# First expert weights sent in three earlier pieces, router sums in column groups, first gather on token rows: one change to a hybrid decoder step

## The chip, the cores and the metric

The kernel runs on one core of one Trainium2 chip. The metric is the device time of one launch, in microseconds (us), as the median of several runs. Engine names are those of the profile: PE is TensorE's matmul, PEld its weight load, DVE is VectorE, ACT is ScalarE, POOL is GpSimd, SP is SyncE; SPq is SP's queue, from which the large DMA transfers are issued.

## The reference

The reference is one layer of a decoder on 288 tokens (256 prompt tokens, 8 sequences of 4 sample tokens), width 1024, all in float32. Attention and a state-space block run side by side, an output projection joins them, and a mixture of 32 experts follows, of which each token uses four:

```
merged = concat[_rmsnorm(attn, ...), _rmsnorm(ssm_o, ...)]
x = x + merged @ lp['w_out']
xn2 = _rmsnorm(x, lp['norm_ffn_g'])
y_ff = _moe(xn2, w_router, b_router, w_gate_up, b_gate_up, w_down, b_down)
x = x + y_ff
...
logits = x2d @ w_router + b_router          # 32 experts
top_v, top_i = lax.top_k(logits, TOP_K)     # 4 of them
gates = softmax(top_v)
h = xb @ w_gate_up[e] + b_gate_up[e]        # 1024 -> 2048
out = _clamped_swiglu(h) @ w_down[e] + b_down[e]
```

The expert weights are 32 x (8 MB + 4 MB), and every one of them is read once in a launch.

## The kernel before, in words

Each engine has its own list of instructions, written out by hand in program order; semaphores (`wait_ge`, `then_inc`) are all that ties the lists together. Nothing reorders them.

**First part.** Activations stand transposed in `xT` (8 tiles of 128 channels x 288 tokens). PE makes the input projection, attention (`score`, `turn`, `values`) and the state-space block (`outputs(0)` to `outputs(3)`). Then come three stretches of 32 matmuls each: the first half of `w_out` on the attention half, `w_glu`, and the second half of `w_out` ("outB", eight tiles m = 0 to 7). For each outB tile DVE scales and adds (`v_rot`, `xT`, `xg`, lines 1676 to 1679) and ACT squares the new `xT` tile into `x2sq`; PE adds the squares up through a matrix of ones (`square(k)`, one matmul after each tile, in bank 4).

**Router.** After the last tile PE makes the logits: `w_r` is the moving operand, the tokens are the stationary one (3 token blocks of 96 x 8 channel tiles). The mean square is turned into 1/rms on all 128 rows (`r2`), transposed to token rows (`rt`), and the token-row copies `x_tok` of the normalised input are made by transposes and ACT copies. DVE picks the four best experts of each token (`lg`, `v8`, `eq`, `sel`), PE counts places (`pos_ready`), DVE builds `oh`, the 0/1 matrix of the tokens of the first expert, and PE gathers those tokens (`gather_first`). After `oh`, DVE goes on with the order in which the experts are to be processed (`ord_e`, semaphore `order_ready`).

**Experts.** Each of 32 experts is processed once, on 64 or 32 token slots ("mid" 64, "few" 32, "many" 64 and 32). Weights come in blocks of 1 MB: 8 blocks of gate/up weights in `gu_ring` and 4 of down weights in `dn_ring`, whose 8 slots hold two experts. `gate_up` uses the gate/up blocks one after the other and gives each slot free with `gu_used`; `down` does so with `dn_used`.

**SP's queue** sets when weights are sent. `load_first` sends the first 16 blocks (all of `gu_ring` and `dn_ring`) once `glu_done` has reached 8, because the rings lie on memory that the first part uses. `load_others` waits for `order_ready`, reads three expert numbers, and then sends the remaining 368 blocks one by one, each when its slot is free: for the first of them SP waits for `gu_used` >= 1. SP issues in program order, so a wait holds up everything behind it.

The profile's lines of `mm` all read L474 (its only `matmul` call); groups are told apart by the tiles they read.

## Time and profile before

| | |
|---|---|
| median of 3 runs | 1167.56 us (1161.33 to 1170.48) |
| time of the profiled execution | 1161.27 us |
| its span, first to last instruction | 1159.4 us |
| mean granted TensorE clock | 0.968 |
| PE busy | 1042.1 us (90%) |
| DVE busy | 411.0 us (35%) |
| ACT busy | 200.9 us (17%) |
| read from HBM | 419.86 MB |

The page gives busy times per engine, the span in 40 slices, the chain that ended last, and groups of instructions. The first sixth of the span is the first part and the router; the rest is the 32 experts. A busy share is no bound by itself: here PE and the DMA engines are both nearly full through the experts, and what matters is which of them waits for the other.

### The profile page before, as it was taken

The page shows a single profiled execution, that of the slowest core. Times are in us where ns is not written, and L with a number is a line of the kernel's source. Part 1 is how long each engine was busy: PE and PEld are TensorE (multiplying, and loading weights), DVE is VectorE, ACT ScalarE, POOL GpSimd, SP SyncE. Part 2 cuts the span into 40 slices and gives each one's busy share as a digit, 9 for nine tenths or more (in the row PEclk, how much of TensorE's full clock was granted, in tenths as well). Part 3 has the DMA queues.
Part 4 walks back from the last instruction along what each step waited for, and adds up shares of the span by engine and source line. Part 5 has one row for each costly group of instructions (what it writes and reads, how often), then busy time and mean ns, then how long its engine had stood idle before and what let it go on. Part 6 is the DMA issues. An engine that isn't in the chain of part 4 may idle for free.

```text
span 1159.4 us, 17080 instructions
## 1 busy us (share of the span) xinstructions
PE 1042.1 (90%) x6475; PEld 448.8 (39%) x6475; DVE 411.0 (35%) x886; ACT 200.9 (17%) x425; POOL 2.7 (0%) x6
## 2 busy tenths in 40 slices
PE   6977899999998999889988998879999999999995
PEld 5755777533233323332332233223333333333332
DVE  6898525323132313231323122223333333222223
ACT  3296423011011101110111111011111111111110
POOL 0000000000000000000000000000000000000000
PEclk9966999799999999999999999999999999999997
DMA  9511039799999999999999999999999999999994
GB/s 360 158 42 73 7 124 423 295 377 421 420 395 422 421 421 422 422 421 422 422 422 421 422 422 421 421 421 421 420 421 421 421 423 422 421 423 421 422 421 186
DMA packets 63303, 425.01 MB, mean 367 GB/s; under 512 B 8196, under 2 KB 10884, under 8 KB 13344
## 3 DMA queue, kind: packets, MB, share of 16 engines
q1 hardware_dynamic: 61488, 422.23, 88.5%
q10 hardware_dynamic: 1728, 2.11, 0.5%
q8 instruction: 25, 0.41, 0.1%
q0 software_dynamic: 48, 0.15, 0.0%
q14 instruction: 14, 0.11, 0.0%
HBM read 419.86 MB, written 2.51 MB: 364 GB/s over the span
## 4 chain that ended last, share of the span: by engine, by line
PE 76%; DVE 9%; DMA 9%; issue 3%; ACT 2%; SPq 1%; ACTq 1%; DVEq 0%
PE banks L474 72%; DMA gu_ring<-w_gu_dram 9%; DVE xT L1813 2%; DVE raw L1767 1%; PE banks L824 1%; PE banks L786 1%; ACT gath L1209 1%; PE banks L877 1%; DVE hl L1779 1%; DVE hT L1784 1%; SPq L319 1%; PE banks L884 0%; PE banks L831 0%; ACT raw_s L1253 0%; DVE hl L1776 0%
## 5 line engine op out<-in xcount | busy, mean ns | idle before, releaser
L474 PE MATMUL banks<-gu_ring,xe 128*64 128x512 f32 x1408 | 324.5, 603 | 4.9 <-DMA gu_ring<-w_gu_dram 4.2
L1813 DVE TENSOR_TENSOR xT<-xT,banks 128x576 f32<-128x576 f32 x132 | 93.6, 751 | 487.6 <-PE banks L474 487.6
L474 PEld LDWEIGHTS banks<-gu_ring,xe 128*64 128x64 f32 x1408 | 95.2, 138 | 198.9 <-issue 182.5
L474 PE MATMUL banks<-dn_ring,hT 128*64 128x512 f32 x704 | 157.7, 596 | 3.5 <-DVE hT L1784 3.5
L474 PE MATMUL banks<-gu_ring,xe_s 128*32 128x512 f32 x896 | 110.6, 600 | 7.4 <-DMA gu_ring<-w_gu_dram 7.4
L474 PEld LDWEIGHTS banks<-dn_ring,hT 128*64 128x64 f32 x704 | 47.9, 137 | 94.6 <-issue 88.7
L474 PE MATMUL banks<-gT,ye 64*128 64x288 f32 x352 | 57.8, 439 | 12.7 <-DVE xT L1813 12.7
L1224 ACT ACTIVATE raw<-banks 128x512 f32<-128x512 f32 x22 | 13.1, 597 | 294.4 <-PE banks L474 294.4
L474 PE MATMUL banks<-x_tok,oh 96*64 96x512 f32 x252 | 58.7, 601 | 0.0
L474 PE MATMUL banks<-dn_ring,hT_s 128*32 128x256 f32 x896 | 55.6, 396 | 2.7 <-ACT xe_s L1243 2.7
L1767 DVE COPY raw<-banks 128x512 f32<-128x512 f32 x22 | 15.2, 692 | 107.4 <-PE banks L474 107.4
L474 PEld LDWEIGHTS banks<-gu_ring,xe_s 128*32 128x32 f32 x896 | 22.2, 108 | 76.5 <-issue 58.3
L474 PEld LDWEIGHTS banks<-gT,ye 64*128 64x128 f32 x352 | 28.7, 185 | 49.9 <-DVE xT L1813 29.3
L1233 ACT ACTIVATE ye<-banks 128x512 f32<-128x512 f32 x22 | 13.1, 597 | 159.2 <-PE banks L474 159.2
L474 PEld LDWEIGHTS banks<-dn_ring,hT_s 128*32 128x32 f32 x896 | 28.0, 113 | 31.5 <-issue 17.4
L474 PE MATMUL banks<-xg,w_in 128*128 128x288 f32 x160 | 39.8, 406 | 0.0
L474 PE MATMUL banks<-aT,w_out 128*128 128x288 f32 x128 | 34.0, 420 | 3.3 <-issue 3.3
L474 PE MATMUL banks<-gT_s,ye_s 32*128 32x288 f32 x224 | 22.1, 464 | 15.7 <-DVE xT L1813 15.1
L474 PEld LDWEIGHTS banks<-xg,w_in 128*128 128x128 f32 x160 | 30.4, 190 | 8.4
L824 PE MATMUL banks<-ident,raw 128*128 128x128 f32 x176 | 28.9, 287 | 4.7 <-DVE raw L1767 4.7
L474 PEld LDWEIGHTS banks<-aT,w_out 128*128 128x128 f32 x128 | 25.1, 198 | 10.6 <-issue 3.6
L824 PEld LDWEIGHTS banks<-ident,raw 128*128 128x128 f32 x176 | 18.4, 140 | 27.8 <-issue 18.0
(338 smaller groups left out, 858.9 us busy)
## 6 DMA issues: line engine op xcount, KB each, us to landing
gu_ring<-w_gu_dram SPq DMA_DIRECT2D x256, 1024.0 KB, 24.0
dn_ring<-w_dn_dram SPq DMA_DIRECT2D x128, 1024.0 KB, 21.9
w_out<-w_out_dram SPq DMA_DIRECT2D x2, 2048.0 KB, 7.9
w_in<-w_in_dram SPq DMA_DIRECT2D x3, 1024.0 KB, 15.9
w_in<-w_in_dram SPq DMA_DIRECT2D x4, 512.0 KB, 10.2
W<-W1c SPq DMA_DIRECT2D x16, 128.0 KB, 2.3
w_glu<-w_glu_dram SPq DMA_DIRECT2D x1, 2048.0 KB, 8.5
xT<-xT_dram SPq DMA_DIRECT2D x2, 576.0 KB, 5.6
```

Source lines behind the costliest of these rows:

```text
L319: sp.dma_start(gu_ring[k][:], a["w_gu"][bass.ds(x, 1), k].rearrange("o p f -> (o p) f")).then_inc(gu_in[k], 16)
L474: return nc.tensor.matmul(out, lhsT, rhs, start=start, stop=stop, **kw)
L786: last = pe.transpose(pb[6][:, c * P:(c + 1) * P], gath[:, c * P:(c + 1) * P], ident[:])
L824: last = pe.transpose(pb[2 + part][:, c * P:(c + 1) * P], raw[:, part, c * P:(c + 1) * P], ident[:])
L877: last = pe.transpose(pb[7][:, t * MT:(t + 1) * MT], goh[0:MT, t], ident[0:MT, 0:MT])
L1209: A(gath[:], pb[5][:], ACT.Copy).then_inc(S("gath_ready"), 1)
L1224: A(raw[:, 0], pb[0][:], ACT.Copy).then_inc(S("g_copied"), 1)
L1233: A(ye[:], pb[4][:], ACT.Copy, scale=0.5).then_inc(S("ye_ready"), 1)
L1767: X.tensor_copy(raw[:, 1], pb[1][:]).then_inc(S("l_copied"), 1)
L1779: X.scalar_tensor_tensor(out=hl[:], in0=hl[:], scalar=1.0, in1=hg[:], op0=ALU.add, op1=ALU.mult).then_inc(S("h_step"), 1)
L1784: X.scalar_tensor_tensor(out=hT[:], in0=th[:], scalar=1.0, in1=hl[:], op0=ALU.add, op1=ALU.mult).then_inc(S("h_ready"), 1)
L1813: X.tensor_tensor(two, two, pair[(1, 3)[n % 2]].rearrange("p (h f) -> p h f", h=2)[:, :, 0:T], ALU.add).then_inc(S("acc_done"), 1)
```

## The change

Four things are moved or written anew.

1. **Loads.** The first 16 blocks go in three pieces: six gate/up blocks when `an_ready` is 4 (the attention half is normalised), four down blocks behind the load of the second half of `w_out`, and the last six (two gate/up, four down) where all 16 went before.
2. **Router.** Squares and logits become matmuls with a 32-column stationary operand, each in one of four column groups of the array (`tile_position`); the partial sums of the four groups lie in the four row quarters of banks 4 and 7. They are done in two halves, after tile 5 and after tile 7. The logits' moving operand is now `xg`. ACT copies the sums to `sumT`, DVE the logits to `lgT`, and matmuls with `fold` (a 0/1 matrix) add the four quarters and turn the result to token rows in one step. 1/rms is then taken on 96 x 3 numbers instead of 128 x 288.
3. **First gather.** `gather_first` is gone; the first expert uses the same `gather(0)` and `turn_gathered(0)` as the later ones: 12 matmul passes on token rows, an ACT copy to `gath`, four transposes, an ACT copy to `xe`.
4. **Fillers and setup.** `busy(bank, src, n)` issues n matmuls whose result nobody reads: 4 ahead of `outputs(0)`, 2 ahead of the first gather, 1 ahead of its transposes and 1 after them. DVE's constants for the experts (12 small instructions) are made before the outB tiles instead of after them.

```
+        sp.wait_ge(S("an_ready"), CT)
+        first_gu(sp, range(0, 6))
         sp.wait_ge(S("outA_done"), KT)
         sp.dma_start(w_out[:], a["w_out"][:, CT:2 * CT]).then_inc(S("wout_in"), 16)
+        sp.wait_ge(S("y_done"), 4)
+        sp.wait_ge(S("hlast_ready"), 2)
+        first_dn(sp, 0)
 
         sp.wait_ge(S("glu_done"), 8)
         sp.wait_ge(S("out_done"), 64)
-        load_first(sp)
+        first_gu(sp, range(6, 8))
+        first_dn(sp, 1)
...
+        def busy(bank, src, n):
+            for _ in range(n):
+                mm(pb[bank][:, 0:src.shape[1]], ident[:], src, True, True)
...
+        busy(4, xT[:, 0, 0:2 * P], 4)
         pe.wait_ge(S("tz_ready"), 16)
         pe.wait_ge(S("hin_ready"), 2)
         outputs(0)
...
-        def square(k):
-
-            if k == 0:
+        def router_part(h):
+
+            def square(q):
+                pe.wait_ge(S("x2sq_ready"), 4 * h + q + 1)
+                return mm(pb[4][NE * q:NE * q + NE, 0:T], ones[:, 0:NE], x2sq[:, q], h == 0, h == 1,
+                          tile_position=(0, NE * q))
+
+            def logit(q):
+                k, g = 4 * h + q, (q + 1) % 4
+                pe.wait_ge(S("xn_ready"), k + 1)
+                return mm(pb[7][NE * g:NE * g + NE, 0:T], w_r[:, k], xg[:, k], h == 0, h == 1, tile_position=(0, NE * g))
+
+            if h == 0:
                 pe.wait_ge(S("sv_ready"), 1)
...
-            if m >= 2:
-                square(m - 2)
-        square(KT - 2)
-        square(KT - 1)
+            if m == 5:
+                router_part(0)
+        router_part(1)
...
-        for t, (f, n) in enumerate(MTS):
-            for k in range(KT):
-                last = mm(pb[5][0:n, t * NE:(t + 1) * NE], xg[:, k, f:f + n], w_r[:, k], k == 0, k == KT - 1)
+        def fold_rows(bank, src, n):
+            for t, (f, w) in enumerate(MTS):
+                last = mm(pb[bank][0:w, t * n:(t + 1) * n], src[:, f:f + w], fold[:, 0:n], True, True)
             last.then_inc(S("logits_ready"), 1)
...
         pe.wait_ge(S("xtok_ready"), 6)
+        busy(0, xg[:, 0, 0:2 * P], 2)
...
-        gather_first()
+        gather(0)
+        busy(0, xg[:, 0, 0:2 * P], 1)
+        turn_gathered(0)
+        busy(0, xg[:, 0, 0:2 * P], 1)
```

On SP's queue, from the load of `w_glu` to the wait for the expert order. Before:

```order
L438 DMA w_glu<-w_glu_dram 128x4096 [waits x_ready]
L440 DMA w_out<-w_out_dram 128x4096 [waits outA_done]
L328 DMA gu_ring_49<-w_gu_dram 128x2048 [waits out_done,glu_done]
L328 DMA gu_ring_50<-w_gu_dram 128x2048
L328 DMA gu_ring_51<-w_gu_dram 128x2048
```

After:

```order
L442 DMA w_glu<-w_glu_dram 128x4096 [waits x_ready]
L330 DMA gu_ring_49<-w_gu_dram 128x2048 [waits an_ready]
L330 DMA gu_ring_50<-w_gu_dram 128x2048
L330 DMA gu_ring_51<-w_gu_dram 128x2048
L330 DMA gu_ring_52<-w_gu_dram 128x2048
L330 DMA gu_ring_53<-w_gu_dram 128x2048
L330 DMA gu_ring_54<-w_gu_dram 128x2048
L446 DMA w_out<-w_out_dram 128x4096 [waits outA_done]
L335 DMA dn_ring_57<-w_dn_dram 128x2048 [waits hlast_ready,y_done]
```

Six expert blocks now stand ahead of `w_out`'s second half and four behind it.

On PE, from the end of outB to the expert's first gather. Each row's tiles are written banks<-moving or stationary operands, the shape is that of the result. Before:

```order
L474 MATMUL banks<-aT,w_out 128x288 x3
L474 MATMUL banks<-x2sq,ones 128x288 [waits x2sq_ready] x3
L474 MATMUL banks<-w_r,xg 96x32 [waits xn_ready,late_in]
L474 MATMUL banks<-w_r,xg 96x32 x23
L732 MATMUL banks<-ident,r_156 96x128 [waits r2_ready]
L732 MATMUL banks<-ident,r_156 96x128 x2
L742 MATMUL banks<-ident,xg 96x128 [waits x2_ready]
L742 MATMUL banks<-ident,xg 96x128 x15
```

After:

```order
L484 MATMUL banks<-aT,w_out 128x288 x3
L484 MATMUL banks<-x2sq,ones 32x288 [waits x2sq_ready] x3
L484 MATMUL banks<-xg,w_r 32x288 [waits xn_ready] x3
L484 MATMUL banks<-x2sq,ones 32x288 [waits x2sq_ready]
L484 MATMUL banks<-xg,w_r 32x288 [waits xn_ready]
L767 MATMUL banks<-ident,xg 96x128 [waits x2_ready]
L767 MATMUL banks<-ident,xg 96x128 x3
L484 MATMUL banks<-fold,sumT 96x1 [waits r2sum_ready]
L484 MATMUL banks<-fold,sumT 96x1 x2
L767 MATMUL banks<-ident,xg 96x128 x4
L484 MATMUL banks<-fold,lgT 96x32 [waits x2v_ready]
```

The 24 logit matmuls behind the last square are gone; two short folds stand among the transposes, and one of them waits for an ACT copy, the other for a DVE copy.

On PE, around the first gather, after:

```order
L484 MATMUL banks<-sel,ones 128x32 x3
L484 MATMUL banks<-xg,ident 128x256 [waits xtok_ready]
L484 MATMUL banks<-xg,ident 128x256
L484 MATMUL banks<-x_tok_159,oh 64x512 [waits oh_ready]
L484 MATMUL banks<-x_tok_159,oh 64x512
L484 MATMUL banks<-x_tok_160,oh 64x512 x2
L484 MATMUL banks<-x_tok_161,oh 64x512 x2
L484 MATMUL banks<-xg,ident 128x256
L809 MATMUL banks<-ident,gath 128x128 [waits gath_ready]
L809 MATMUL banks<-ident,gath 128x128 x3
L484 MATMUL banks<-xg,ident 128x256
L484 MATMUL banks<-gu_ring_49,xe 64x512 [waits gu_in0,xe_ready]
```

Six matmuls of 512 columns stand where 24 of 64 columns stood, with a copy and four transposes behind them and the fillers (`xg,ident`) in the gaps.

## Rows read from the trace of the kernel before

**Rows 1.** The page, the span in 40 slices: GB/s moved.

```profile
GB/s 360 158 42 73 7 124 423 295 377 421 420 395 422 421 421 422 422 421 422 422 422 421 422 422 421 421 421 421 420 421 421 421 423 422 421 423 421 422 421 186
```

**Rows 2.** Windows: stretch, length, busy per engine, granted clock, DMA share, GB/s.

```profile
214.00:216.00 2.00, 2.00 (x6) 0.47 (x4) 0.00 (x0) 0.00 (x0) 0.00 (x0) 0.50 0.00 0
...
217.00:220.00 3.00, 3.00 (x17) 1.03 (x15) 0.00 (x0) 0.41 (x1) 0.00 (x0) 0.95 0.57 150
...
230.00:240.00 10.00, 9.09 (x46) 3.37 (x44) 5.05 (x11) 3.70 (x5) 0.00 (x0) 1.00 0.96 369
240.00:250.00 10.00, 10.00 (x49) 3.35 (x47) 0.00 (x0) 1.01 (x2) 0.00 (x0) 1.00 0.87 342
...
330.00:340.00 10.00, 10.00 (x103) 3.71 (x102) 0.38 (x2) 0.87 (x2) 0.00 (x0) 1.00 0.91 343
...
400.00:1130.00 730.00, 669.61 (x4212) 236.42 (x4216) 208.56 (x410) 85.22 (x167) 0.00 (x0) 1.00 1.01 422
```

**Rows 3.** Timeline of SP's queue: start, duration, line, transfers issued.

```profile
153.14 0.34 SPq L440 DMA_DIRECT2D w_out<-w_out_dram  x1
168.66 4.09 SPq L328 DMA_DIRECT2D gu_ring<-w_gu_dram  x8
...
217.29 16.17 SPq L319 DMA_DIRECT2D gu_ring<-w_gu_dram  x8
```

**Rows 4.** SP's waits from 205 to 219 us: total, times, longest.

```profile
SPq L352 <- DVE ord_e L1834: 21.9, 1, 21.9
SPq L319 <- PE banks L474: 4.2, 1, 4.2
```

**Rows 5.** Timeline of PE up to outB: start, duration, passes (two per float32 matmul).

```profile
119.35 0.43 PE L474 MATMUL banks<-pT,v_tok 32*64 32x128 f32 x2
...
119.71 0.44 PE L474 MATMUL banks<-U,Tz 128*128 128x72 f32 x2
...
152.94 15.68 PE L474 MATMUL banks<-yT,w_glu 128*128 128x288 f32 x64
...
184.52 0.65 PE L474 MATMUL banks<-x2sq,ones 128*128 128x288 f32 x2
...
185.00 2.10 PE L474 MATMUL banks<-aT,w_out 128*128 128x288 f32 x8
```

**Rows 6.** The page's groups: busy, mean ns of one, idle before.

```profile
L474 PE MATMUL banks<-gu_ring,xe_s 128*32 128x512 f32 x896 | 110.6, 600 | 7.4 <-DMA gu_ring<-w_gu_dram 7.4
```

**Rows 7.** Timeline from the last outB tile to the first gather.

```profile
189.57 0.46 DVE L1676 TENSOR_TENSOR v_rot<-banks,v_rot 128x288 f32<-128x288 f32 x1 [1.07 <-PE banks L474]
...
190.55 0.44 ACT L1189 ACTIVATE x2sq<-xT 128x288 f32<-128x288 f32 x1 [1.98 <-DVE xT L1677]
...
191.84 0.46 DVE L1682 TENSOR_SCALAR r<-banks 128x288 f32<-128x288 f32 x1 [0.91 <-PE banks L474]
...
195.66 0.51 PE L732 MATMUL banks<-ident,r 128*96 128x128 f32 x3
...
196.47 0.56 DVE L1705 SCALAR_TENSOR_TENSOR lg<-banks,rt,cols 96x32 f32<-96x32 f32 x3
...
202.43 0.35 DVE L1738 TENSOR_TENSOR oh<-iota,pos 96x192 f32<-96x192 f32 x1
...
202.93 9.80 PE L474 MATMUL banks<-oh,x_tok 96*128 96x64 f32 x48 [1.24 <-DVE oh L1738]
```

**Rows 8.** The same timeline, the expert order and the first expert.

```profile
211.23 0.18 DVE L1834 CAST ord_e<-more 128x32 int32<-128x32 f32 x1
...
213.42 5.57 PE L474 MATMUL banks<-gu_ring,xe 128*64 128x512 f32 x16 [0.69 <-ACT xe L1300]
```

**Rows 9.** Timeline: gather, copy, transposes and copy of the second expert.

```profile
234.33 2.79 PE L474 MATMUL banks<-x_tok,oh 96*64 96x512 f32 x12
...
237.17 0.60 ACT L1209 ACTIVATE gath<-banks 128x512 f32<-128x512 f32 x1 [1.05 <-PE banks L474]
...
238.52 0.60 ACT L1214 ACTIVATE xe<-banks 128x512 f32<-128x512 f32 x1 [0.75 <-PE banks L786]
```

More of the change, by code:

```diff
@@ L180, in build @@
     par_t = [sb(f"par_t{k}", [NPAR], W16 + 3 * sz(NPAR) + k * sz(NPAR)) for k in range(11)]
-    x2sq = sb("x2sq", [2, T], WK)
-    r2 = sb("r2", [T], WK + 2304)
+    x2sq = sb("x2sq", [4, T], WK)
+    lgT = sb("lgT", [T], WK + 9600)
+    sumT = sb("sumT", [T], WK + 10752)
+    fold = sb("fold", [NE], WK + 13952)
     o = W16
@@ L323, in load_dn, with first_gu, first_dn @@
         sp.dma_start(dn_ring[k][:], a["w_dn"][bass.ds(x, 1), c].rearrange("o p k f -> (o p) k f")).then_inc(dn_in[k], 16)
-    def load_first(sp):
-        for k in range(8):
+    def first_gu(sp, slots):
+        for k in slots:
             sp.dma_start(gu_ring[k][:], a["w_gu"][0, k]).then_inc(gu_in[k], 16)
-        for j in range(2):
-            for c in range(4):
-                sp.dma_start(dn_ring[4 * j + c][:], a["w_dn"][j, c]).then_inc(dn_in[4 * j + c], 16)
+    def first_dn(sp, j):
+        for c in range(4):
+            sp.dma_start(dn_ring[4 * j + c][:], a["w_dn"][j, c]).then_inc(dn_in[4 * j + c], 16)
     def load_others(sp):
@@ L697, in _ @@
         last.then_inc(S("bdn_turned"), 1)
-        def square(k):
-            if k == 0:
-                pe.wait_ge(S("sv_ready"), 1)
-            pe.wait_ge(S("x2sq_ready"), k + 1)
-            mm(pb[4][:, 0:T], ones[:], x2sq[:, k % 2], k == 0, k == KT - 1).then_inc(S("x2sum_ready"), 1)
+        def router_part(h):
[8 more added lines that the diff above has]
+            if h == 0:
+                pe.wait_ge(S("sv_ready"), 1)
+            for q in range(3):
+                square(q)
+            for q in range(3):
+                logit(q)
+            square(3).then_inc(S("x2sum_ready"), 1)
+            last = logit(3)
+            if h == 1:
+                last.then_inc(S("logits_ready"), 1)
         pe.wait_ge(S("sn_ready"), CT)
@@ L743, in _ @@
             last.then_inc(S("xtok_turned"), 1)
+            if u == 0:
+                pe.wait_ge(S("r2sum_ready"), 1)
+                fold_rows(4, sumT, 1)
+            if u == 1:
+                pe.wait_ge(S("x2v_ready"), 1)
+                fold_rows(5, lgT, NE)
         pe.wait_ge(S("sel_ready"), 1)
-        pe.wait_ge(S("x2v_ready"), 1)
+        pe.wait_ge(S("x2v_ready"), 2)
         for t in range(3):
@@ L761, in gather @@
                               t == 0, t == 2, tile_position=(0, SLOTS * h))
-            last.then_inc(S("gathered"), 1)
-        def gather_first():
-            pe.wait_ge(S("oh_ready"), 1)
-            for k in range(KT):
-                f = (k % 4) * P + (k // 4) * SLOTS
-                for t in range(3):
-                    last = mm(pb[6][:, f:f + SLOTS], x_tok[t][0:MT, k * P:(k + 1) * P], oh[0:MT, t], t == 0, t == 2)
             last.then_inc(S("gathered"), 1)
@@ L1184, in _ @@
             act.wait_ge(S("x2_ready"), k + 1)
-            if k >= 2:
-                act.wait_ge(S("x2sum_ready"), k - 1)
+            if k == 4:
+                act.wait_ge(S("x2sum_ready"), 1)
             if k == 0:
                 act.wait_ge(S("sn_ready"), CT)
-            A(x2sq[:, k % 2], xT[:, k], ACT.Square).then_inc(S("x2sq_ready"), 1)
-        rsqrt(r2[:], r2[:], r2[:], [("x2v_ready", 1)], "r2_ready")
+            A(x2sq[:, k % 4], xT[:, k], ACT.Square).then_inc(S("x2sq_ready"), 1)
+        act.wait_ge(S("x2sum_ready"), 2)
+        A(sumT[:], pb[4][:, 0:T], ACT.Copy).then_inc(S("r2sum_ready"), 1)
+        rsqrt(rt[0:MT], rt[0:MT], rt[0:MT], [("x2v_ready", 2)], "rt_ready")
         act.wait_ge(S("bdn_turned"), 1)
@@ L1297, in act_expert @@
                 act_result_s(p)
-        act.wait_ge(S("gathered"), 1)
-        A(xe[:].rearrange("p c h s -> p (c h s)"), pb[6][:], ACT.Copy).then_inc(S("xe_ready"), 1)
+        act_gathered(0)
+        act_turned(0)
         act_expert(0, 0, 0, KINDS[0], "bias", KINDS[1])
@@ L1698, in _ @@
         link(X.tensor_copy(iota2[:, 1], iota[:, 0:SLOTS]))
-        M = slice(0, MT)
-        dve.wait_ge(S("logits_ready"), 4)
-        X.tensor_copy(rt[M], pb[5][M, P:4 * P:P]).then_inc(S("rt_ready"), 1)
+        dve.wait_ge(S("sr_ready"), 1)
+        dve.wait_ge(S("xmid_ready"), KT)
+        for m in range(KT):
+            dve.wait_ge(S("outB_done"), m + 1)
+            link(X.tensor_tensor(v_rot[:, 1], pb[m % 4][:, 0:T], v_rot[:, 0], ALU.mult))
+            X.tensor_tensor(xT[:, m], xT[:, m], v_rot[:, 1], ALU.add).then_inc(S("x2_ready"), 1)
+            dve.wait_ge(S("x2_ready"), m + 1)
+            X.tensor_scalar(xg[:, m], xT[:, m], col(C_GFFN + m), None, ALU.mult).then_inc(S("xn_ready"), 1)
+        M = slice(0, MT)
+        dve.wait_ge(S("logits_ready"), 1)
+        X.tensor_copy(lgT[:], pb[7][:, 0:T]).then_inc(S("x2v_ready"), 1)
+        dve.wait_ge(S("logits_ready"), 2)
+        X.tensor_scalar(rt[M], pb[4][M, 0:3], 1 / D, EPS, ALU.mult, ALU.add).then_inc(S("x2v_ready"), 1)
+        dve.wait_ge(S("logits_ready"), 3)
         dve.wait_ge(S("rt_ready"), 1)
```

23 lines of the change are left out of this document (4 added, 19 removed).

## The prediction, made before the changed kernel was run

> **What bounds the kernel now.** I began with the slices of the page [rows 1]. From the tenth slice on the chip moves 420 to 423 GB/s almost without a break; only the twelfth slice, and the ones ahead of the tenth, are lower. The windows say the same: 422 GB/s over the 730 us from 400 to 1130 us [rows 2]. One block of weights is 1.049 MB, so it takes 2.49 us, and the 368 blocks behind the first 16 take 386 / 0.422 = 914 us. The expert part is a stream of transfers, and the kernel ends when the stream has ended and the last expert is done. So a change to the first part is worth what it moves that stream.
>
> What sets the stream's place? SP's timeline shows the first 16 blocks issued from 168.66 us and the next one only at 217.29 [rows 3]; in between there is a stretch with 0 GB/s [rows 2]. SP's waits say why [rows 4]: it waited for the expert order until about 211.4 (the last instruction of it ends at 211.23 + 0.18 [rows 8]), and then 4.2 us more for PE, for the first slot of `gu_ring`. PE started the first expert at 213.42 [rows 8]. A slot is free after 8 passes; at half clock (granted clock 0.50, that is 1.2 GHz [rows 2]) these are half of the 16 passes of 5.57 us and more, some 3.5 us, and end at about 217. So **PE, not the order, releases the stream**, and SP was ready at 217.1 - 4.2 = 212.9.
>
> After that the stream is held up three more times: 369, 342 and 343 GB/s in the windows from 230, 240 and 330 us [rows 2]. Against 422 that is 10 x (1 - 369/422) = 1.3, 1.9 and 1.9 us, 5.1 us in all. There too the ring has no free slot: PE is late. After 340 us the stream is never held up again. So the end moves with PE as long as PE is the later of the two at those places, and it can move at most by (SP's start moved + 5.1 us).
>
> **Part by part: PE up to the first expert.**
>
> (a) *Filler ahead of `outputs(0)`.* PE goes from the attention's last matmul (119.35 + 0.43 with its drain) to the first of `outputs` at 119.71 without idling [rows 5], so nothing hides the filler. A pass of 288 columns takes (185.00 - 184.52) / 2 = 0.24 us [rows 5], one of 256 columns 0.21; four matmuls are 8 passes: **+1.7 us**. All that follows on PE is a chain of its own results up to outB, so it is passed on in full.
>
> (b) *outB with squares.* Five full squares ahead of the last tile go, 5 x 0.48 = 2.4 us. Eight small matmuls come in, 16 passes. Where four column groups are used now, 896 passes of 512 columns take 110.6 us [rows 6], 0.123 us each; for 288 columns 0.069, so 16 x 0.069 = 1.1 us. Bounds: 0.5 (hidden between tiles) and 16 x 0.24 = 3.9 (no overlap). Taken: 1.1, since that row is the same kind of matmul. **-1.3 us.**
>
> (c) *From the last tile to the logits on token rows.* Before: DVE starts on the last tile at 189.57 and makes `lg` at 196.47, 6.9 us [rows 7]. After: two DVE steps and the ACT square as now, up to 190.55 + 0.44 (1.4 us); the square's sum until the next engine reads it, 191.84 - 191.0 = 0.8; ACT's copy 0.5; the fold of the sums (three tiny matmuls), of which PE is held for about 0.4; four transposes 0.5; the fold of the logits with its latency about 0.7, by the three transposes at 195.66 that DVE could use at 196.3 [rows 7]. Sum 4.3, so **-2.6 us**. Beside it run the DVE scaling and ACT's two small steps for 1/rms. Bounds: -1.5 to -3.5. DVE's 12 setup instructions leave a place where they were hidden for another where DVE waits for ACT's 1/rms and then for tiles that come 1.9 us apart, while its own work per tile is 1.3 us: nothing.
>
> (a) to (c): -2.2 us. `oh` moves from 202.43 to 200.2, the order's end from 211.4 to 209.2.
>
> (d) *First gather.* Before: 202.93 to 213.42, 10.5 us, at half clock for most of it [rows 7, 8]. After: as for the second expert, from 234.33 until `xe` is written at 238.52 + 0.60, 4.8 us [rows 9]. The fillers (0.43 us for each matmul) lie in PE's waits for `oh` and for the two copies. **-5.7 us.** This price holds at full clock only.
>
> (e) *Clock of the first blocks.* The 16 passes at 213.42 took 5.57 us [rows 8]. The second expert's gather makes 12 of the same size in 2.79 us at full clock [rows 9], so 16 take 3.7, of which the drain at the end is 0.2: 3.5. **-2.0 us**, if the clock stays up.
>
> PE sum: -2.2 - 5.7 - 2.0 = **-9.9 us**; I take -9.5 for passes and semaphore delays that I can't see.
>
> **The stream.** SP is ready at 212.9 - 2.2 = 210.7; the first slot is free at about 213.4 - 7.9 + 2.0 = 207.5. Now it is the order that releases the stream, at 210.8 instead of 217.3: -6.5 us. With all 5.1 us of later holdups gone it could gain 11.6 us. PE is the later one, so the gain is PE's, 9.5 us.
>
> *The early loads.* By themselves they remove no wait: before, the first gate/up block was in place long ahead of 213 us. What they cover is the rest of the change. 16 blocks take 39.8 us; sent all from 168.7 + 1.7 they would be in at about 212, 1 to 2 us after SP is ready for the next. Early, the ring is full at about 187. Cost: six blocks (15 us) from about 138 us end at 153, just as `w_out`'s second half is issued (153.14 + 1.7 [rows 3]); it takes 5 us and is needed at about 172. Does a full stream slow PE? w_glu ran with hardly a transfer beside it, 64 passes in 15.68 us, 0.245 each; outB ran under a full stream at 0.24 [rows 5]. No: the cost is nothing.
>
> The Trainium skill, in "DMA: Bandwidth & Descriptors" (Where 436 GB/s comes from), gives about 358 GB/s as what binds a transfer from HBM. The window of 422 GB/s [rows 2] contradicts it for a single core; with 358 the six blocks would take 17.6 us, still ahead of 172.
>
> **The rivals.**
>
> *The clock falls again* (chance 0.2). Before, TensorE fell to half its clock during the first gather, after a few us of small matmuls and waits, and stayed there until the first expert had run a while [rows 2, 7]. After, the stretch from the last transpose to the filler is no shorter: about 3 us of waits and 32-column matmuls. For it: the fillers are only 0.85 us ahead of the gather. Against: what follows is 512-column matmuls, as in the experts, where the clock is 1.00. Then the gather takes 2.8 us more, transposes and fillers 0.6, and the 2.0 us of (e) are lost: -9.5 + 5.4 = -4.1 us. The Trainium skill, "TensorE: Matmul & The Clock Gate", says that the throttled state is the default and activity releases it; the fall in these rows agrees, and by that rule either outcome is open here.
>
> *More is gained* (0.17). With (b) hidden and the folds short, PE is no longer the later one and the order's path gains as well: up to the 11.6 us above plus 1, about -12 us.
>
> *The column groups don't overlap* (0.08). Square and logit matmuls of different groups follow each other with waits between; then part 0 costs 3.9 instead of 1.1, part 1 about 1.5 more: -9.5 + 4.3 = -5.2 us. The Trainium skill, "TensorEngine Tiling (Array Packing)" (Key Properties), says that changing the tiling mode drains TensorE; each part brings two such changes. The row has no price for it.
>
> *Slower: the weights stand in front of `w_out`* (0.05). Its second half is issued behind six blocks. If the stream ran so slowly in this stretch that `w_out` were not in at 172, outB and everything behind it would wait. 2.1 + 6.3 = 8.4 MB from 138 us: the gain of 9.5 us is used up when they are in at 181.5, at 193 GB/s, and at 170 GB/s the kernel is about 6 us slower. Against: 420 GB/s wherever a stream of blocks runs [rows 1].
>
> **How the numbers follow.** The forecast, -9.5 us, has a chance of 0.5: span 1159.4 - 9.5 = 1149.9, time 1161.3 - 9.5 = 1151.8 for an execution like the profiled one. That one was at the low end of the three runs shown, 6.3 us below their median; a stream of fixed length loses the same microseconds in any of them, so the predicted median is 1167.6 - 9.5 = 1158. One per cent is 11.7 us, about what a measurement of this kernel tells from no change. The range reaches from the larger gain in a run like the faster ones (1152) to the case of the fallen clock and a little more (1165). Faster by over 1%: the larger gain and the part of the forecast that reaches it by the bounds of (b) and (c), 0.3. Slower by over 1%: 0.04. Within: 0.66.
>
> **What the changed profile would show.** The first block behind the ring issued at about 211 us, and SP's last wait before it is for the order, not PE; the first expert's matmuls from about 205.5 at clock 1.00; `lg` at about 194.3; no window under 415 GB/s from 230 to 250 us. I am wrong if the outB tiles start less than 1.5 us later than 170.8, if the clock is 0.50 at the gather, or if the windows after 220 us show the stream waiting elsewhere.

## The result, and the profile after

| | before | after |
|---|---|---|
| median of 10 runs each | 1166.24 us (1161.33 to 1170.48) | 1157.16 us (1155.93 to 1162.10) |
| time of the profiled execution | 1161.27 us | 1155.93 us |
| its span | 1159.4 us | 1154.1 us |
| mean granted TensorE clock | 0.968 | 0.975 |

The changed kernel takes 0.9927 of the time of before, with a 95% interval of 0.9905 to 0.9948: 8.5 us less by this ratio, 9.1 us between the medians. The forecast was 9.5 us less and a median of 1158. The two profiled executions differ by only 5.3 us, and neither number is the sum of the steps as I had them: two things that I had not seen, one for the change and one against it, nearly cancelled. That the median came so near to the forecast is luck.

**The start of the stream.** SP's queue after: start, duration, transfers issued.

```profile
135.37 3.35 SPq L330 DMA_DIRECT2D gu_ring<-w_gu_dram  x6
...
153.35 2.09 SPq L335 DMA_DIRECT2D dn_ring<-w_dn_dram  x4
168.44 0.80 SPq L330 DMA_DIRECT2D gu_ring<-w_gu_dram  x2
...
209.29 5.69 SPq L321 DMA_DIRECT2D gu_ring<-w_gu_dram  x5
```

SP's waits from 197 to 219 us: total, times, longest.

```profile
SPq L356 <- DVE ord_e L1863: 34.8, 1, 34.8
SPq L321 <- PE banks L484: 2.5, 3, 1.1
```

The first block behind the ring goes at 209.29 instead of 217.29 [rows 3]: -8.0 us. Where the 4.2 us for PE stood [rows 4] there are short waits of at most 1.1 us, and those come after the first blocks. The order releases the stream now, as forecast.

**PE and DVE from the last outB tile to the first expert.** The timeline after, DVE's and PE's rows.

```profile
188.25 0.46 DVE L1720 TENSOR_TENSOR v_rot<-banks,v_rot 128x288 f32<-128x288 f32 x1 [0.58 <-PE banks L484]
...
192.55 0.56 DVE L1734 SCALAR_TENSOR_TENSOR lg<-banks,rt,cols 96x32 f32<-96x32 f32 x3 [0.78 <-PE banks L484]
...
198.57 0.35 DVE L1767 TENSOR_TENSOR oh<-iota,pos 96x192 f32<-96x192 f32 x1
...
207.37 0.18 DVE L1863 CAST ord_e<-more 128x32 int32<-128x32 f32 x1
```

```profile
197.64 2.06 PE L484 MATMUL banks<-xg,ident 128*128 128x256 f32 x4
199.63 3.45 PE L484 MATMUL banks<-x_tok,oh 96*64 96x512 f32 x12
...
203.78 0.66 PE L809 MATMUL banks<-ident,gath 128*128 128x128 f32 x4
204.27 0.60 PE L484 MATMUL banks<-xg,ident 128*128 128x256 f32 x2
205.12 3.65 PE L484 MATMUL banks<-gu_ring,xe 128*64 128x512 f32 x16 [0.25 <-ACT xe L1242]
```

From the last tile to the logits it is 192.55 - 188.25 = 4.3 us, against 6.9 [rows 7]. From `oh` to the first expert it is 6.55 us, against 10.99 [rows 7, 8]. The 16 passes take 3.65 us, against 5.57 [rows 8].

**Windows after**: stretch, length, busy per engine, granted clock, DMA share, GB/s.

```profile
197.60:201.00 3.40, 3.40 (x10) 1.73 (x11) 2.87 (x10) 0.00 (x0) 0.00 (x0) 0.50 0.00 0
```
```profile
210.00:220.00 10.00, 9.16 (x52) 3.13 (x50) 2.84 (x4) 0.00 (x0) 0.00 (x0) 1.00 0.96 386
...
230.00:240.00 10.00, 10.00 (x51) 3.36 (x49) 0.00 (x0) 1.01 (x2) 0.00 (x0) 1.00 0.95 338
...
320.00:330.00 10.00, 10.00 (x98) 3.42 (x96) 1.82 (x8) 0.60 (x2) 0.00 (x0) 1.00 0.84 318
...
400.00:1130.00 730.00, 670.26 (x4208) 236.46 (x4200) 206.06 (x402) 84.08 (x165) 0.00 (x0) 1.00 1.01 421
```

The clock falls to 0.50 for 3.4 us, over the fillers and the first 1.4 us of the gather, and is back before the first expert. The stream is still held up twice, by 10 x (1 - 338/422) = 2.0 and 10 x (1 - 318/422) = 2.5 us; right behind its start, from 210 us, another 0.9 us is missing at 386 GB/s.

**Something new.** I laid the starts of the 32 experts' gate/up matmuls of both traces side by side. After minus before (the experts are counted from 0; I call a negative number a lead) it is -10.2 us at expert 1, -8.6 at expert 5, then -6.4, -5.0, -2.9, even +0.5 at expert 14, and -3.7 at expert 31. The lead is lost between 380 and 620 us, where the change touches nothing. The page's table of DMA queues (packets, MB, share) and PE's waits from 210 to 1140 us (total, times, longest) have a line each that stands out. Before has no wait of PE for "issue" there. The instruction packets, before and then after:

```profile
q8 instruction: 25, 0.41, 0.1%
```
```profile
q8 instruction: 51, 0.84, 0.3%
```

PE's wait, after:

```profile
PE banks L484 <- issue: 8.6, 5, 2.1
```

"Issue" says that PE waits for nothing that the profile shows; with the 26 additional packets beside it I took it that PE waits for its own instructions. Where it does so, the timeline of PE after shows (passes at the row's end, idle before in brackets):

```profile
378.81 1.89 PE L484 MATMUL banks<-dn_ring,hT 128*64 128x512 f32 x8
382.80 1.92 PE L484 MATMUL banks<-gu_ring,xe_s 128*32 128x512 f32 x16 [2.11 <-issue]
384.65 0.47 PE L900 MATMUL banks<-ident,goh 96*128 96x96 f32 x3
385.05 1.92 PE L484 MATMUL banks<-gu_ring,xe_s 128*32 128x512 f32 x16
388.13 1.06 PE L484 MATMUL banks<-gu_ring,xe_s 128*32 128x512 f32 x8 [1.16 <-issue]
```

At 382.80 us begins the first pass of the second turn of PE's loop over experts 2 to 17 (four turns of four experts); the other stops lie at the next two turns. The DMA table of the window from 379 to 497 us, which is one turn, shows the packets of the kernel after:

```profile
q8 instruction: 9, 0.15, 0.5%
```

The two turns behind it (497 to 617 and 617 to 738 us) have nine each as well. From 400 to 740 us the kernel before has none. So the first theory to test was this one: the change removed about 80 instructions ahead of the loop, and the loop now lies in a place of the list where it has to be fetched anew at each turn.

I count places in instructions ahead of the loop, from the program: four for a float32 matmul (two weight loads, two passes), two for a transpose (one load, one pass), one for most others. The loop is then 1664 instructions long, and it stands at 2505 before and at 2425 after. The expectations below were written with another count, which takes a transpose as four too: 1778 for the loop, 2721 before and 2643 after. The pages decide between the two. They have 6475 passes before and 6436 after, exactly what the program comes to with one pass for a transpose; with two it would be 7010 and 6972. Within one kernel a shift is the same by either count, but kernels with different numbers of transposes ahead of the loop are compared rightly by the first one alone, and that settles one of the cases below.

### The profile page after: what moved, and what is told of

It is laid out like the page before. It is cut to its first block, busy times and chain, and to the rows that moved or that the text cites. A ratio compares the mean times of both kernels' runs of the same rounds, so it can differ in the third digit from the quotient of the medians.

```text
span 1154.1 us, 16996 instructions
## 1 busy us (share of the span) xinstructions
PE 1034.8 (90%) x6436; PEld 437.5 (38%) x6436; DVE 410.9 (36%) x887; ACT 201.2 (17%) x427; POOL 2.7 (0%) x6
## 4 chain that ended last, share of the span: by engine, by line
PE 78%; DVE 10%; DMA 5%; issue 4%; ACT 2%; SPq 1%; ACTq 1%; DVEq 0%
PE banks L484 74%; DMA gu_ring<-w_gu_dram 5%; DVE xT L1842 2%; DVE raw L1796 1%; PE banks L847 1%; PE banks L809 1%; ACT gath L1237 1%; SPq L321 1%; PE banks L900 1%; DVE hl L1808 1%; DVE hT L1813 1%; PE banks L854 1%; ACT raw_s L1281 0%; DVE G_rot L1538 0%; PE banks L907 0%
## 5 line engine op out<-in xcount | busy, mean ns | idle before, releaser
L484 PE MATMUL banks<-gu_ring,xe_s 128*32 128x512 f32 x896 | 111.7, 608 | 10.2 <-issue 8.6
L484 PE MATMUL banks<-x_tok,oh 96*64 96x512 f32 x264 | 62.2, 606 | 0.0
L484 PE MATMUL banks<-xg,w_in 128*128 128x288 f32 x160 | 39.8, 406 | 0.0
## 6 DMA issues: line engine op xcount, KB each, us to landing
dn_ring<-w_dn_dram SPq DMA_DIRECT2D x128, 1024.0 KB, 18.7
```

The costliest lines, as they stand in the source:

```text
L484: return nc.tensor.matmul(out, lhsT, rhs, start=start, stop=stop, **kw)
```

## The experiments

The place is set with `n` matmuls of one column behind `outputs(3)`, where PE waits for the attention's norm anyway, and up to four waits that are already fulfilled (the four come to two instructions in the list):

```
         outputs(2)
         outputs(3)
+        for name in ("hin_ready", "tz_ready", "k_ready", "pv_ready")[:w]:
+            pe.wait_ge(S(name), 1)
+        for _ in range(n):
+            mm(pb[4][0:NE, 0:1], ident[:, 0:NE], xT[:, 0, 0:1], True, True)
```

Behind each median stands its ratio to the kernel before as measured beside it, with the 95% interval. The median of before was 1167.7, 1167.1 or 1165.0 us in the three groups of runs, so kernels of different groups are compared by their ratios.

### The loop's place

**a_pad**: the changed kernel, n = 19, w = 4 (loop at 2503; 2721 in the count of the expectations).

> The changed kernel with 19 one-column matmuls and four waits that are already fulfilled, all on PE behind outputs(3), where PE waits for the attention's norm. The work is the same; PE's expert loop then starts at the same place in PE's list of instructions (2721 instructions of 64 bytes ahead of it) as in the kernel before, instead of 2643. Theory H (the 26 additional instruction packets and the five idle times of 2 us ahead of loop turns in the changed kernel come from where the loop lies in the list): about 25 packets on the instruction queue instead of 51, no idle time put down to issue between 385 and 630 us, and 3 to 5 us less than the changed kernel, so 12 us under the kernel before. Rival R1 (the packets depend on something else, such as the total length or the state of the chip): 51 packets again and the time of the changed kernel, 8 to 9 us under before. Rival R2 (the packets go, but the stream of weights covers the idle times): 25 packets, and the time of the changed kernel within 1 us.

Measured: 1153.85 us, 0.9879 (0.9857 to 0.9901), an interval wholly under that of the changed kernel. Its page and its timeline at the same turn:

```profile
q8 instruction: 24, 0.39, 0.1%
```
```profile
379.71 2.74 PE L484 MATMUL banks<-dn_ring,hT 128*64 128x512 f32 x12
382.38 1.92 PE L484 MATMUL banks<-gu_ring,xe_s 128*32 128x512 f32 x16
384.24 0.47 PE L904 MATMUL banks<-ident,goh 96*128 96x96 f32 x3
384.63 2.78 PE L484 MATMUL banks<-gu_ring,xe_s 128*32 128x512 f32 x24
```

No stop, and the lead over before is -6.8 us at expert 5 and at expert 31. More work gives less time. R1 and R2 are out.

**b_shift**: the kernel before, n = 10, w = 0 (loop at 2545).

> The kernel before with 10 one-column matmuls (40 instructions) behind outputs(3), in PE's wait for the attention's norm; nothing else is changed. The expert loop starts 40 instructions later in PE's list, at 2761. H: about 51 instruction packets instead of 25, idle times put down to issue at the loop's turns, and 1 to 5 us more than the kernel before. R1: 25 packets, no difference. R2: 51 packets, no difference in time.

Measured: 1166.19 us, 0.9997 (0.9973 to 1.0021), 25 packets, no stops. R1's numbers, so H as I had put it, "the place of before or else", is too narrow: 2545 (2761 in its expectation) is good as well.

**b_gather_new** (its main subject is below) came with a surprise: at 2721 by the count that I used then, the place of before, it had 51 packets and stops of up to 7.7 us, and was slower than before. That called for four runs on the place alone.

**b_gather_761**: the same kernel, 10 more of the one-column matmuls (loop at 2537).

> b_gather_new (the kernel before with the new first gather alone) with 10 more one-column matmuls behind outputs(3): the expert loop starts 2761 instructions into PE's list, where b_shift had 25 packets, instead of 2721. b_gather_new led the kernel before by 3.5 us until the loop's first turn and then lost 17 us in three stops of 7.7 us with 51 instruction packets. If the place of the loop decides: 25 packets, no stops, and the 3.5 us stay: 4 us under before, about 1163. If something else in this kernel causes the fetches: 51 packets and about 1177 again.

Measured: 1162.59 us, 0.9952 (0.9928 to 0.9976), 25 packets, no stops, against 1.0090 forty instructions earlier: ten useless matmuls are worth 1.4% here.

**a_761**: the changed kernel, n = 29, w = 4 (loop at 2543).

> The changed kernel with 29 one-column matmuls and four fulfilled waits behind outputs(3): loop start at 2761 instead of 2721 as in a_pad or 2643 as in the changed kernel. If the place decides and the good stretch reaches from 2721 to 2761: 24 or 25 packets and a_pad's time, 1153 to 1155. If a_pad was a lucky case of something else: 51 packets and 1157 or more. The padding lies in PE's wait for the attention's norm and costs nothing in either case.

Measured: 1153.10 us, 0.9899 (0.9862 to 0.9936), 25 packets, no stops. a_pad was no lucky case. These two have the lowest medians of all.

**a_half**: the changed kernel, n = 10, w = 0 (loop at 2465).

> The changed kernel with 10 one-column matmuls behind outputs(3): loop start at 2683, half way between the changed kernel (2643, 51 packets) and a_pad (2721, 24 packets). If the place decides, one of the two outcomes with nothing between: 51 packets and about 1157, or 24 and about 1154; which one tells on which side the border lies.

Measured: 1161.59 us, 0.9970 (0.9948 to 0.9992), 51 packets. Neither outcome that I expected: slower than both. Its PE timeline at the loop's turn:

```profile
382.81 1.92 PE L484 MATMUL banks<-gu_ring,xe_s 128*32 128x512 f32 x16 [2.18 <-issue]
388.27 0.46 PE L902 MATMUL banks<-ident,goh 96*128 96x96 f32 x3 [3.54 <-issue]
```

**a_tail**: the changed kernel with the 19 matmuls behind the last combine, so the list is as long as a_pad's and the loop stays at 2425.

> The changed kernel with 19 one-column matmuls behind the last combine, ahead of the wait for list_ready: PE's list is as long as a_pad's, and the expert loop stays at 2643. If the place of the loop decides: 51 packets, idle times put down to issue at the loop's turns, and the changed kernel's time or up to 1 us more for the 19 matmuls at the end. If the length of the list decides: 24 packets and about 1154.

Measured: 1157.36 us, 0.9933 (0.9902 to 0.9963), 51 packets, 8.9 us of stops. The length of the list doesn't decide it.

What these runs say together (idle for issue and leads over before from each profile):

| kernel | loop at | in the count of the expectations | packets | idle for issue | lead at expert 5 | at expert 31 |
|---|---|---|---|---|---|---|
| after | 2425 | 2643 | 51 | 8.6 us | -8.6 | -3.7 |
| a_late (below) | 2425 | 2643 | 51 | 10.1 | -8.6 | -3.7 |
| a_tail | 2425 | 2643 | 51 | 8.9 | -7.5 | -2.6 |
| a_half | 2465 | 2683 | 51 | 15.8 | -8.6 | +0.5 |
| b_gather_new | 2497 | 2721 | 51 | 22.5 | -3.5 | +13.0 |
| a_pad | 2503 | 2721 | 24 | 0 | -6.8 | -6.8 |
| a_gather_old (below) | 2511 | 2721 | 25 | 0 | +0.6 | +0.4 |
| b_gather_761 | 2537 | 2761 | 25 | 0 | +2.4 | +2.2 |
| a_761 | 2543 | 2761 | 25 | 0 | -7.7 | -7.8 |
| b_shift | 2545 | 2761 | 25 | 0 | 0.0 | +0.4 |

Before and b_loads (2505, 25 packets) and a_nofill_out and a_nofill_gather (2503, 24 packets) have no such stops either.

(b_gather_761's profiled execution came 7 us late to w_glu, as the last section of experiments shows; what counts is that it loses nothing between the two columns.)

The rows fit a list fetched in pieces of 16 KB, 256 instructions of 64 bytes: the whole list has 24.5 to 25 such pieces, and a kernel without stops has 24 or 25 packets. Three profiles give the place of a border between two pieces. In the changed kernel PE makes 16 + 3 + 16 = 35 passes between its two stops; with their weight loads and three other instructions that is 73, so a piece ends at 2425 + 73 = 2498. In a_half it is 16 passes and two others: 2465 + 34 = 2499. In b_gather_new the first pass of the loop is late already, behind two other instructions: 2497 + 2 = 2499. The closer the loop's start stands ahead of this border, the sooner the second piece is missed behind the first, and the more of the two fetches is bare: 2.1 + 1.2, then 2.2 + 3.5, and then 7.4 us in one. From 2503 on there are no stops. So what parts b_gather_new (2497) from a_pad (2503) is the same border; by the count of the expectations they stood at one place. Why a start behind the border spares the fetch the runs alone don't say.

The Trainium skill, "Runtime: NRT & Kernel Launch" (Instruction fetch mechanics), gives PE a first-in-first-out store of 128 KB, which is 2048 instructions, refilled in blocks of 16 KB. The trace agrees with the size of a block: 0.41 MB in 25 packets. The same section also speaks of a window of only two pages, and says that a taken branch to a target outside of it has to wait for a fetch. The runs contradict the two pages: in a_pad a loop of 6.5 pieces turns without a packet. By the first figure eight pieces are there at a time, and then the rows can be understood. Begun behind the border the loop lies in seven pieces, eight with the next one in line; begun ahead of it, it lies in eight, and the next one is the ninth, and nine is the number of packets in each turn. I argue this from the page; no run here shows the store itself.

### The early loads

**b_loads**: the kernel before, with SP's list of the changed kernel and nothing else.

```
+        sp.wait_ge(S("an_ready"), CT)
+        first_gu(sp, range(0, 6))
         sp.wait_ge(S("outA_done"), KT)
...
+        sp.wait_ge(S("y_done"), 4)
+        sp.wait_ge(S("hlast_ready"), 2)
+        first_dn(sp, 0)
...
-        load_first(sp)
+        first_gu(sp, range(6, 8))
+        first_dn(sp, 1)
```

> The kernel before with the three earlier pieces of loads alone: SP's list is that of the changed kernel, PE, DVE and ACT have the lists of before. Prediction's step (the early loads by themselves remove no wait): within 1 us of before, the first block behind the ring still issued at about 217 us, released by PE. Rival (the first blocks were late for the first expert, or 40 us of transfers less in the stretch from 168 to 212 us free something else): 2 us or more faster, and the first expert's matmuls start earlier than 213.4 us. Rival (w_out's second half comes late behind six blocks): the outB tiles start later than 170.8 us, slower by that.

Measured: 1164.65 us, 0.9987 (0.9967 to 1.0007). Alone they do nothing that shows, and SP still waits for PE, 4.8 us, ahead of its first block behind the ring. The profiled execution was among the longest, 1170.24 us, and shows outB 6.2 us late. The section on the filler ahead of `outputs(0)` says why, and it isn't the loads: b_gather_761, with the loads of before, has the same delay.

**a_late**: the changed kernel, all 16 blocks at `glu_done` 8.

```
-        sp.wait_ge(S("an_ready"), CT)
-        first_gu(sp, range(0, 6))
...
-        first_gu(sp, range(6, 8))
-        first_dn(sp, 1)
+        first_gu(sp, range(0, 8))
+        first_dn(sp, 0)
+        first_dn(sp, 1)
```

> The changed kernel with all 16 first blocks sent where the kernel before sends them (glu_done 8); PE, DVE and ACT are as in the changed kernel. Prediction's step (the early loads cover 1 to 2 us of the rest of the change): the 16 blocks are in at about 168.4 + 39.8 = 208.2 plus the entries, while SP is ready at 209.3, so 0 to 2 us slower than the changed kernel, 6.5 to 8.5 us under before. Rival (the early loads are worth nothing even beside the rest): the time of the changed kernel. Rival (they carry the gain, because the first expert at 205.1 needs gate/up blocks and its down blocks while the queue still works): 4 us or more slower than the changed kernel, with waits of PE for gu_ring or dn_ring from 205 to 225 us.

Measured: 1158.19 us, 0.9925 (0.9903 to 0.9947), beside 0.9927 for the changed kernel. SP's queue in a_late:

```profile
172.36 14.43 SPq L335 DMA_DIRECT2D dn_ring<-w_dn_dram  x8
186.84 2.13 SPq L452 DMA_DIRECT2D entries<-entries_dram  x1
209.47 7.09 SPq L321 DMA_DIRECT2D gu_ring<-w_gu_dram  x5
```

The issue of the eight down blocks takes 14 us, beside work, and the stream goes on 0.2 us later than in the changed kernel. The three early pieces, the largest part of the diff on SP, are worth less than a measurement can tell. Both kernels of this pair have the loop's stops; beside a_pad the early loads were not taken out.

### The first gather and its fillers

**b_gather_new**: the kernel before with `gather(0)`, its transposes and the four filler matmuls around them; n = 10, w = 2 (loop at 2497).

```
         pe.wait_ge(S("xtok_ready"), 6)
+        busy(0, xg[:, 0, 0:2 * P], 2)
...
-        gather_first()
+        gather(0)
+        busy(0, xg[:, 0, 0:2 * P], 1)
+        turn_gathered(0)
+        busy(0, xg[:, 0, 0:2 * P], 1)
```

> The kernel before with the new first gather alone (gather(0), turn_gathered(0), the four fillers around them); loads, router and all else as before, expert loop at its place. Prediction's steps: PE's first expert at 213.42 - 5.7 = 207.7 and its first slot free at about 210; then the order releases the stream, which SP takes up at 212.9 instead of 217.3, -4.4 us; time 4 to 5 us under before. Rival (without the earlier loads the first gate/up blocks are late now, since 16 blocks from 168.7 us on come in order and the eighth is in at 189): waits of PE for gu_ring at the first expert and less than 2 us gained. Rival (half clock stays in spite of the fillers, since the stretch ahead of the gather is longer here, with the transposes of r2 and the old logits): passes of the first expert at 0.5, 2 us or less gained.

Measured: 1177.04 us, 1.0090 (1.0065 to 1.0115). Up to the loop's turn it gains, but less than forecast. Here outB starts 1.1 us later, and the clock was at half for most of the gather, which took 5.03 us: the first expert starts at 211.81 us, not 207.7, and SP goes on at 214.42, not 212.9, after a last wait of 1.6 us for PE. Experts 1 to 5 lead before by 3.5 us. Then this, in its PE timeline, and twice more:

```profile
382.51 3.17 PE L474 MATMUL banks<-dn_ring,hT 128*64 128x512 f32 x14
393.11 2.79 PE L474 MATMUL banks<-gu_ring,xe_s 128*32 128x512 f32 x12 [7.43 <-issue]
```

Of 22.5 us of such stops, 16.5 reach the end. PE waits for `gu_ring` for 1.1 us in all here, and 11.6 before: the rest of the stops lies where PE would have waited for weights. With the loop moved (b_gather_761) the kernel gains 0.5%, some 5.6 us, against 4 to 5 expected.

**a_gather_old**: the changed kernel with the gather of before and without the fillers around it; n = 9, w = 2 (loop at 2511), 25 packets.

```
-        gather(0)
-        busy(0, xg[:, 0, 0:2 * P], 1)
-        turn_gathered(0)
-        busy(0, xg[:, 0, 0:2 * P], 1)
+        gather_first()
```

> The changed kernel with the first gather of the kernel before (24 matmuls with x_tok as the stationary operand, one ACT copy) and without the fillers around it; expert loop at the place of before. Prediction's steps (d) and (e): 5.7 + 2.0 us of PE are given back: the first expert's matmuls start about 6 us later than in a_pad, at 212.5 to 213, at half clock, the first block behind the ring goes at 216.5 to 217 by PE's release, 6 us later than in a_pad, and the time is 5 to 6 us above a_pad, about 1159.5. Rival (the stream's later holdups give it back, or the order is what counts): 2 us or less above a_pad.

Measured: 1160.01 us, 0.9943 (0.9923 to 0.9963): 6.2 us above a_pad. Gather, first expert and first block behind the ring in a_gather_old, and then in a_pad:

```profile
200.82 10.47 PE L484 MATMUL banks<-oh,x_tok 96*128 96x64 f32 x48 [1.24 <-DVE oh L1776]
211.99 5.95 PE L484 MATMUL banks<-gu_ring,xe 128*64 128x512 f32 x16 [0.69 <-ACT xe L1337]
215.85 2.64 SPq L321 DMA_DIRECT2D gu_ring<-w_gu_dram  x2
```
```profile
201.26 3.60 PE L484 MATMUL banks<-x_tok,oh 96*64 96x512 f32 x12
206.90 3.65 PE L484 MATMUL banks<-gu_ring,xe 128*64 128x512 f32 x16 [0.25 <-ACT xe L1246]
211.01 5.75 SPq L321 DMA_DIRECT2D gu_ring<-w_gu_dram  x5
```

SP's start moves by 4.8 us, PE's second expert by 9.0, the end by 7.2 in the profiles. The router is new in both, so this is the part of the gather and its fillers together.

**a_nofill_gather**: the changed kernel without the four fillers at the gather; n = 23, w = 2 (loop at 2503), 24 packets.

```
-        busy(0, xg[:, 0, 0:2 * P], 2)
...
-        busy(0, xg[:, 0, 0:2 * P], 1)
...
-        busy(0, xg[:, 0, 0:2 * P], 1)
```

> The changed kernel without the four filler matmuls around the first gather (2 ahead of it, 1 ahead of the transposes, 1 behind them), expert loop at the place of before. To be compared with a_pad (gather at 201.26, first expert's matmuls at 206.90, SP's first block behind the ring at 210.95). Theory (they hold the clock): granted clock 0.5 from about 200 us over gather, transposes and the first expert's first passes; the passes start at about 210.3 and take 5.6 us instead of 3.7, PE instead of the order releases the stream, at about 214; 3 us slower than a_pad. Rival (they do nothing, the clock comes back by itself or the few matmuls don't matter): the half-clock stretch is as in a_pad (3.4 us) and the time within 1 us of a_pad.

Measured: 1156.35 us, 0.9897 (0.9872 to 0.9923), 2.5 us above a_pad's median; the intervals overlap, so it is the profile that decides:

```profile
199.92 5.39 PE L484 MATMUL banks<-x_tok,oh 96*64 96x512 f32 x12 [1.24 <-DVE oh L1768]
...
207.79 5.88 PE L484 MATMUL banks<-gu_ring,xe 128*64 128x512 f32 x16 [0.69 <-ACT xe L1243]
```
```profile
200.00:212.00 12.00, 10.62 (x26) 3.22 (x28) 8.40 (x13) 1.19 (x2) 0.00 (x0) 0.50 0.01 1
```

Half clock all through 200 to 212 us. The same passes take 5.39 and 5.88 us instead of 3.60 and 3.65; the second expert's lead over before is 3.6 us instead of 8.4. In this execution the fillers' absence costs the clock. SP goes on at 211.66 us, not at 214 as expected: its order was ready 0.9 us earlier than a_pad's, and PE then held it for 1.6 us. Two of the six times (1151.8 and 1152.6 us) are as short as a_pad's, so it isn't shown that the clock stays down in every execution without the fillers.

### The filler ahead of `outputs(0)`

**a_nofill_out**: the changed kernel without it; n = 23, w = 4 (loop at 2503), 24 packets.

```
-        busy(4, xT[:, 0, 0:2 * P], 4)
```

> The changed kernel without the filler ahead of outputs(0), its expert loop at the place of the kernel before (23 one-column matmuls and four fulfilled waits behind outputs(3)). To be compared with a_pad (1153.85 us). Prediction's step (a): the filler costs 1.7 us where PE comes to it late, and nothing where values ran at full clock and PE waits for DVE anyway; so 0 to 1.7 us faster than a_pad, about 1.3. Rival (the filler keeps the clock up in the stretches behind it): half-clock stretches in outputs, w_glu or outB that a_pad's profile doesn't have, single times spread over 10 us as those of the kernel before (1159 to 1170), and a median 1 to 4 us above a_pad.

Measured: 1157.98 us, 0.9905 (0.9873 to 0.9936). Its six times are 1151.1, 1151.9, 1156.5, 1159.5, 1159.6 and 1159.8, those of a_pad 1152.1 to 1154.9. The two intervals overlap, so the difference of the medians is no more than likely. The profiled one (1159.47) is one of the long ones; PE's timeline and a window show what happens in it:

```profile
116.69 0.43 PE L484 MATMUL banks<-pT,v_tok 32*64 32x128 f32 x2
119.28 0.41 PE L484 MATMUL banks<-U,Tz 128*128 128x72 f32 x2 [2.16 <-DVE r_scan L1552]
```
```profile
119.00:132.00 13.00, 12.72 (x54) 12.04 (x55) 3.10 (x8) 2.68 (x4) 0.66 (x1) 0.52 0.04 13
```

The attention's `values` ran at full clock here, so PE was done early, idled 2.16 us for DVE, and then made `outputs` at half clock for 13 us: w_glu starts at 160.0 instead of a_pad's 154.5 us. In the changed kernel the filler lies in just this gap:

```profile
116.67 0.43 PE L484 MATMUL banks<-pT,v_tok 32*64 32x128 f32 x2
117.03 1.99 PE L484 MATMUL banks<-xT,ident 128*128 128x256 f32 x8
119.26 0.41 PE L484 MATMUL banks<-U,Tz 128*128 128x72 f32 x2 [0.23 <-DVE r_scan L1549]
```

None of the eight profiles with this filler has half clock from 119 to 132 us. Of the six without it three do (this one, b_gather_761, and b_loads, where w_glu starts at 159.1); in the other three, before among them [rows 5], `values` itself ran slowly until 119.7 us, so that PE came late and there was no gap.

## Why the prediction came out right, and where it was wrong

**(a) The filler ahead of outputs(0): wrong, in sign.** "Nothing hides the filler" holds only for an execution in which `values` runs at half clock, as in the one that I read. a_pad's was of that kind, and there w_glu starts 154.50 - 152.94 = 1.6 us later, the 1.7 of the sum (a_gather_old, also of that kind, has the same 1.6). In the changed kernel's own profile w_glu starts 0.2 us earlier than before. And the filler does what I gave it no credit for: without it the next stretch loses some 7 us of clock in part of the executions.

**The step from one execution to the median: wrong.** I wrote that a stream of fixed length loses the same microseconds in any execution. The median fell by 9.1 us, the profiled pair differs by 5.3. The profiled execution of before was among the short ones; many of its others, up to 1170 us, lie as far above it as the profile of b_loads does, and nine of the changed kernel's ten times lie within 2.3 us. That those long executions of the kernel before have this cause is argued from b_loads, whose PE list is the same, and not shown for each.

**(b) outB: right.** From the first outB matmul (170.62) to DVE on the last tile it is 17.6 us, before 189.57 - 170.84 = 18.7: -1.1 against -1.3. The first part of the router's matmuls holds PE from 182.95 to 184.07 us, 1.1 us as in the sum, where matmuls without overlap would take 3.9:

```profile
182.95 0.44 PE L484 MATMUL banks<-x2sq,ones 128*32 128x288 f32 x3
...
184.07 4.15 PE L484 MATMUL banks<-aT,w_out 128*128 128x288 f32 x16
```

The column groups do overlap; that rival is out.

**(c) Last tile to logits: right**, 4.3 us to the decimal, -2.6. No run has the new router alone; (b) and (c) are read from these rows.

**(d) First gather: right in kind, 1.3 us too large.** From `oh` to the first expert -4.4, not -5.7. The clock was at 0.50 when the fillers ahead of the gather ran: they took 2.06 us instead of 0.85 and so outlasted the wait that was to hide them, by 199.63 - 198.92 = 0.7 us, and the gather took 3.45 instead of 2.79.

**(e) Clock of the first blocks: right**, -1.9 against -2.0; I had taken a drain of 0.2 us off the new time and not off the old one, and without that the sum gives 1.9. The rival of the fallen clock came true for 3.4 us only; a_nofill_gather shows it in full.

Sum on PE at expert 1: -10.2 us, against -9.9 added up and -9.5 taken: (a) better by 1.9, (d) worse by 1.3.

**The stream.** SP's start -8.0 us; forecast -6.5, and the difference is again (a): with the filler on the path, in a_pad, it is -6.3. But "PE is the later one, so the gain is PE's" failed. In the changed kernel PE leads by 10.2 us at expert 1 and by 8.6 from expert 4 on, and a_pad, a_761 and the changed kernel keep at expert 5 SP's own move plus 0.5 to 0.6 us. The later holdups didn't shrink: 5.1 us before, about 4.9 after (2.0, 2.5, and 0.4 from 330 to 340 us, at 406 GB/s); my sign "no window under 415 GB/s from 230 to 250" was wrong at 338. Of the three signs by which I wanted to know that I was wrong, the first came in full: outB starts at 170.62 us and not 1.5 us later than before. The other two came in part: the clock was 0.50 for the first 1.4 us of the gather, and the stream still waits after 220 us, in two windows instead of three.

**The early loads: right**, at nothing alone, and less than the 1 to 2 us of cover that I gave them. That figure rested on a wrong sum: 168.7 + 1.7 + 39.8 is 210.2, not 212, and SP was to be ready at 210.7. The slower rival, weights ahead of w_out, is out: w_glu and outB start as before.

**What no step had: the loop's place.** 5 of the 8.6 us of lead at expert 5 are lost at the loop's turns. So the range and the direction held, while the sum lacked one term for (the filler's clock, in the median) and one against (the instruction fetch), of 3 to 5 us each. With the loop past the border the change gives 1.0 to 1.2%.

## What to carry to other kernels

After any change of an engine's program look at the instruction packets on the page: more of them than before, with waits for "issue" at a loop's turns, mean that a loop no longer stays loaded, and a few idle instructions ahead of it, in a place where the engine waits anyway, can bring it back. Count the instructions as the engine gets them, and check the count against the passes on the page. A difference of 1% between two versions of a kernel with loops of this size can be this and nothing of what was changed in the work. And a filler is priced twice: by what it takes where PE is late, and by what the clock does behind the gap where PE is early; one profile shows only one of the two.

## What was not expected of the hardware

- A loop of 1664 PE instructions (104 KB) is fetched anew at each of three turns or not at all, by a shift of 40 instructions: 51 or 25 packets of 16 KB, 22.5 us or none of idle time, 1177.0 or 1162.6 us for the same work.
- The cost grows towards the border and is gone behind it: 8.6 us of idle time at 2425 instructions ahead of the loop, 15.8 at 2465, 22.5 at 2497 and none at 2503, these in kernels that differ in their gathers.
- Work added can shorten a kernel: 19 one-column matmuls and four fulfilled waits, and the median goes from 1157.2 to 1153.9 us.
- 2.16 us of idle PE at 117 us are followed by 13 us at half clock, after which w_glu starts more than 5 us later than in a_pad.
